# Six tiles of an input projection computed as fp32 products inside the stage that follows it

## The reference, cut to what matters

```python
def mixer(x, w_in, ...):               # names shortened
    parts = split(x @ w_in)            # 3360 columns: see below
    # a: spatial gating of two 256-wide parts       -> 256 columns
    # b: gated delta rule, 8 heads of 64, chunked   -> 512 columns
    # c: gated linear attention, 4 heads, chunked   -> 256 columns
    return concat([a, b, c]) @ w_out

def gated_deltanet(qkv, z, beta_logit, decay_logit, conv_w, a_log, dt_bias, norm_g):
    qkv = silu(causal_short_conv(qkv, conv_w))
    ...
    o = gated_delta_rule(q, k, v, log_g, beta)      # (I + L)^-1 per chunk, then a scan over chunks
    o = rms_norm_2(o, norm_g) * silu(z)             # z: 512 columns of x @ w_in
    return o
# the linear attention ends likewise: rms_norm_2(o, gla_norm_g) * silu(r), r: 256 columns of x @ w_in
```

## Time and profile before

| | |
|---|---|
| median of 3 runs | 3900.46 us (3897.31 to 3901.8) |
| the profiled execution | 3902.79 us |
| its span from first to last instruction | 3901.0 us |
| PE busy | 3753.3 us, 96% |
| DVE busy | 2088.4 us, 54% |
| ACT busy | 1354.9 us, 35% |
| granted PE clock, mean | 0.967 |
| DMA | 333.38 MB, mean 85 GB/s |

### The profile page before, as it was taken

One profiled execution on the slowest core, in us unless ns is written; L12 is line 12 of the kernel. 1 busy time (PEld: TensorE's weight loads), 2 busy tenths in 40 slices (PEclk: granted clock), 3 DMA queues, 4 the chain that ended last, 5 costly groups with the idle time before them and its releaser, 6 DMA issues.

```text
span 3901.0 us, 45251 instructions
## 1 busy us (share of the span) xinstructions
PE 3753.3 (96%) x18816; PEld 3126.8 (80%) x18816; DVE 2088.4 (54%) x3698; ACT 1354.9 (35%) x2084; POOL 86.1 (2%) x164
## 2 busy tenths in 40 slices
PE   8997999999999999999999979999999999799998
PEld 5985669999987778888887867888788878687886
...
PEclk9998999999999999999999968999999999789999
...
GB/s 220 151 57 1 22 22 133 125 127 127 106 70 33 38 88 96 97 111 97 97 97 86 85 20 44 92 97 97 86 97 97 97 87 86 29 39 87 97 98 81
DMA packets 92887, 333.38 MB, mean 85 GB/s; under 512 B 11364, under 2 KB 11532, under 8 KB 92428
## 3 DMA queue, kind: packets, MB, share of 16 engines
...
...
## 4 chain that ended last, share of the span: by engine, by line
PE 91%; DVE 5%; ACT 2%; issue 1%; DMA 0%; ACTq 0%; DVEq 0%; SPq 0%
PE PS L537 75%; PE PS L1093 2%; PE PS L539 2%; PE PS L1111 1%; PE PS L1639 1%; PE PS L1451 1%; PE PS L1078 1%; PE PS L994 1%; PE PS L1079 0%; PE PS L1081 0%; DVE H_r L719 0%; DVE XH L891 0%; PE PS L2339 0%; PE PS L2566 0%; PE PS L1422 0%
## 5 line engine op out<-in xcount | busy, mean ns | idle before, releaser
L537 PE MATMUL PS<-arena_r,ring_hi 128*128 128x512 f32 (+1 forms) x6124 | 2062.9, 376 | 22.5 <-DVE H_r L719 19.9
L537 PE MATMUL PS<-arena_r,ring_r 128*128 128x512 f32 (+1 forms) x4652 | 1740.2, 374 | 0.0
L537 PEld LDWEIGHTS PS<-arena_r,ring_hi 128*128 128x128 f32 x6124 | 1144.8, 188 | 203.2 <-issue 27.5
L537 PE MATMUL PS<-H_r,ring_hi 128*128 128x512 f32 (+1 forms) x3180 | 1190.1, 374 | 0.0
L537 PEld LDWEIGHTS PS<-arena_r,ring_r 128*128 128x128 f32 x4652 | 874.7, 188 | 129.1
L383 DVE TENSOR_TENSOR ring_r<-ring,ring_hi 128x1024 fp32r<-128x1024 f32 x514 | 627.1, 1222 | 655.1 <-ACT ring_hi L374 654.6
L374 ACT ACTIVATE ring_hi<-ring 128x1024 fp32r<-128x1024 f32 x514 | 541.4, 1055 | 876.9 <-DMA ring<-weights_dram 869.1
L537 PEld LDWEIGHTS PS<-H_r,ring_hi 128*128 128x128 f32 x3180 | 599.2, 188 | 92.8 <-issue 2.6
L1808 ACT ACTIVATE arena<-PS 128x512 f32<-128x512 f32 x88 | 52.6, 598 | 522.0 <-PE PS L537 522.0
L1257 DVE SCALAR_TENSOR_TENSOR XH<-PS,mods,XH 128x256 f32<-128x256 f32 (+1 forms) x168 | 79.4, 517 | 234.3 <-PE PS L537 219.8
L345 DVE CAST arena_r<-arena 128x512 fp32r<-128x512 f32 (+1 forms) x184 | 74.2, 403 | 196.6 <-ACT arena L1304 193.5
...
## 6 DMA issues: line engine op xcount, KB each, us to landing
...
```

What stands on the lines that cost most here:

```text
L537: ins = pe.matmul(PS[:, o.bank, 0:hi - lo], w[:, 0, :], x, **flags)
```

## The change

The six gate tiles leave `in_plan`, which now has 20 tiles; their weights stand in the stream behind it, ahead of the output projection's. They are never split: PE multiplies the raw fp32 slab with the raw fp32 input `X`, 48 products of 128x128 by 128x512 in each layer (`woven_pe`), in groups of 1 to 7 put between the steps of `form_pe`, `units_pe` and `solve_pe`. ACT copies each finished tile out of PSUM in six places (`woven_act`), and applies Silu in place during the scan (`woven_silu_act`), which needs one table load to Silu and one back. The bank numbers of several steps change so that banks 4, 6 and 7 are free for the new tiles, and some of these steps get a wait for a reader of their new bank. ACT and DVE no longer split the six slabs, and the first slabs of the output projection are split later: two high parts in `units_act`, one at the end of `solve_act`, two low parts at the start of `rec_dve`. The jobs beside the tiles of `in_plan` move to lower numbers. The same bytes are loaded.

```diff
 MIX_ORDER = [0, 1, 6, 7, 2, 3, 4, 5]
+WOVEN_COLS = [(2048, 2560), (3088, 3344)]
+WOVEN_BANKS = (4, 4, 6, 7, 6, 7)
+N_WOVEN = len(WOVEN_BANKS)
...
-                s += ftiles(w, (1408, 1536)) + ftiles(w, (512, 1024)) + ftiles(w, (1536, 2560)) + ftiles(w, (2576, 2832))
-                s += ftiles(w, (3088, 3344)) + ftiles(w, (0, 512)) + ttiles(w, (2832, 3088))
+                s += ftiles(w, (1408, 1536)) + ftiles(w, (512, 1024)) + ftiles(w, (1536, 2048)) + ftiles(w, (2576, 2832))
+                s += ftiles(w, (0, 512)) + ttiles(w, (2832, 3088))
+                for cols in WOVEN_COLS:
+                    s += ftiles(w, cols)
...
+WOVEN_SLABS = {i // SLAB for i, (w, k, c, n) in enumerate(stream()) if w in ("in0", "in1") and any(a <= c < b for a, b in WOVEN_COLS)}
+SPLIT_SLABS = [n for n in range(RAW_SLABS, N_SLABS) if n not in WOVEN_SLABS]
+SPLIT_NUMBER = {n: i + 1 for i, n in enumerate(SPLIT_SLABS)}
...
+        def next_split(n):
+
+            n += 1
+            while n in WOVEN_SLABS:
+                n += 1
+            return n
...
-                Splits.high += 1
+                Splits.high = next_split(n)
...
-            t += [ftile(x_x, LAT, "act", func_act(to_lat(zp[:, m, :]), ACT.Silu)) for m in range(4)]
             t += [ftile(x_x, LAT, "dve", copy_dve(to_lat(d))) for d in (qg, kg)]
-            t += [ftile(x_x, LAT, "act", func_act(to_lat(rg[:, m, :]), ACT.Silu)) for m in range(2)]
             t += [ftile(x_x, LAT, "act", func_act(to_lat(d), ACT.Gelu_apprx_tanh)) for d in (up_[:, 0, :], up_[:, 1, :], vp_[:, 0, :], vp_[:, 1, :])]
             t.append(ttile(x_x, range(NCT, NT), 2, "act", copy_act(lambda lo, hi: vg[:, lo // P - NCT, :])))
             banks.first = 0
+            assert Planned.at // SLAB in WOVEN_SLABS
+            Planned.at += SLAB * N_WOVEN
...
-            t[15]["beside_pe"] = lambda pe: turn_rows_pe(pe, l)
-            t[16]["beside_act"] = lambda act: (turned_rows_act(act), high_rows_act(act))
-            t[17]["beside_pe"] = lambda pe: turn_keys_pe(pe, l)
-            t[18]["beside_dve"] = lambda dve: (key_rows_dve(dve, l), low_rows_dve(dve))
-            t[20]["beside_pe"] = lambda pe: turn_values_pe(pe, l)
-            t[21]["beside_dve"] = value_rows_dve
+            t[14]["beside_pe"] = lambda pe: turn_rows_pe(pe, l)
+            t[15]["beside_act"] = lambda act: (turned_rows_act(act), high_rows_act(act))
+            t[15]["beside_pe"] = lambda pe: turn_keys_pe(pe, l)
+            t[16]["beside_dve"] = lambda dve: (key_rows_dve(dve, l), low_rows_dve(dve))
+            t[17]["beside_pe"] = lambda pe: turn_values_pe(pe, l)
+            t[18]["beside_dve"] = value_rows_dve
             return together(t, 4)
...
+        wv_ready, wv_out = signal("woven_tile_ready"), signal("woven_tile_out")
+        woven_dst = [zp[:, m, :] for m in range(4)] + [rg[:, m, :] for m in range(2)]
+
+        class Woven:
+
+            products = tiles = 0
+
+        def woven_pe(pe, n):
+
+            for _ in range(n):
+                tile, k = divmod(Woven.products, KD)
+                j = tile % N_WOVEN
+                w, last_of_slab = raw_tiles(pe, 1)
+                if k == 0 and WOVEN_BANKS[j] in WOVEN_BANKS[0:j]:
+                    before = max(i for i in range(j) if WOVEN_BANKS[i] == WOVEN_BANKS[j])
+                    pe.wait_ge(wv_out.sem, 2 * (tile - j) + before + 1)
+                ins = pe.matmul(PS[:, WOVEN_BANKS[j], :], w[:, 0, :], X[:, k, CTX:TOK], start=(k == 0), stop=(k == KD - 1))
+                if last_of_slab:
+                    ins.then_inc(wv_ready.sem, 1)
+                    Weights.used.append((wv_ready, tile + 1))
+                Woven.products += 1
+
+        def woven_copied_pe(pe, l, j):
+
+            pe.wait_ge(wv_out.sem, 2 * N_WOVEN * l + j)
+
+        def woven_act(act):
+
+            j = Woven.tiles % N_WOVEN
+            act.wait_ge(wv_ready.sem, Woven.tiles + 1)
+            nc.scalar.activation(woven_dst[j], PS[:, WOVEN_BANKS[j], :], ACT.Copy).then_inc(wv_out.sem, 1)
+            Woven.tiles += 1
+
+        def woven_silu_act(act, l, m):
+
+            if m == 0:
+                act.wait_ge(wv_out.sem, 2 * N_WOVEN * l + N_WOVEN)
+            nc.scalar.activation(woven_dst[m], woven_dst[m], ACT.Silu).then_inc(wv_out.sem, 1)
...
-        OUT_BANKS = (6, 0, 7, 1)
+        OUT_BANKS = (4, 0, 5, 1)
 
         def update_of(c):
 
-            return PS[:, 6 - 4 * (c % 2), 64 * (c // 2):64 * (c // 2) + 64]
+            return PS[:, 4 - 2 * (c % 2), 64 * (c // 2):64 * (c // 2) + 64]
 
...
             ins.then_inc(sg_z.sem, 1)
+            woven_pe(pe, 5)
             pe.wait_ge(sg_sq.sem, sg_sq.next("pe"))
...
             ins.then_inc(sg_t.sem, 1)
+            woven_pe(pe, 7)
             pe.wait_ge(sg_v.sem, sg_v.next("pe"))
...
             ins.then_inc(ga_kt.sem, 1)
+            woven_pe(pe, 1)
+            woven_copied_pe(pe, l, 2)
             pe.wait_ge(sg_tc.sem, sg_tc.next("pe"))
             pe.wait_ge(ga_ktc.sem, ga_ktc.next("pe"))
...
             ins.then_inc(sg_z.sem, 1)
+            woven_pe(pe, 2)
             pe.wait_ge(ga_state.sem, ga_state.next("pe"))
...
                 ins.then_inc(ga_s.sem, 1)
+            woven_pe(pe, 4)
             pe.wait_ge(ga_pt.sem, ga_pt.next("pe", 4))
...
             ins.then_inc(ga_o.sem, 1)
+            woven_pe(pe, 4)
...
         def units_act(act, l):
 
+            woven_act(act)
             act.wait_ge(sg_mean.sem, sg_mean.next("act"))
...
             nc.scalar.activation(kdt, PS[:, 5, :].rearrange("p (a b) -> p a b", a=4), ACT.Copy).then_inc(ga_ktc.sem, 1)
+            woven_act(act)
+            woven_act(act)
+            high_up_to(act, Splits.high + 1)
+            high_up_to(act, Splits.high + 1)
             act.wait_ge(ga_o.sem, ga_o.next("act"))
...
             def beta(p):
-                if p >= 2:
-                    pe.wait_ge(so_kb.sem, so_kb.at("pe", p - 2))
-                spread(pe, PS[:, 4 * (p % 2), :], "selp", P * p, mean_r).then_inc(so_beta.sem, 1)
+                spread(pe, PS[:, 0, :], "selp", P * p, mean_r).then_inc(so_beta.sem, 1)
...
             decays(0)
+            woven_pe(pe, 2)
             for p in range(4):
+                pe.wait_ge(so_kb.sem, so_kb.at("pe", p))
                 if p < 3:
                     beta(p + 1)
-                pe.wait_ge(so_kb.sem, so_kb.at("pe", p))
                 if p >= 1:
...
                 products(p, 3, qkv).then_inc(so_kq.sem, 1)
+                woven_pe(pe, 5 if p == 3 else 3)
...
-        EXP_BANKS = (2, 3, 6, 7)
+        EXP_BANKS = (2, 3, 2, 3)
         EXP_SPREADS = ((0, 1), (), (2,), (3,))
...
                 ins.then_inc(so_y.sem, 1)
+            woven_pe(pe, 1)
             pe.wait_ge(so_T.sem, so_T.next("pe"))
             for g in range(2):
...
                 ins.then_inc(so_z.sem, 1)
+                woven_pe(pe, 2)
                 for p in EXP_SPREADS[r]:
+                    if p == 1:
+                        pe.wait_ge(so_offv.sem, so_offv.at("pe", 1))
+                    if p >= 2:
+                        pe.wait_ge(re_qd.sem, re_qd.at("pe", p - 2))
                     spread(pe, PS[:, EXP_BANKS[p], :], "selp", P * p, exp_r, 64).then_inc(re_eg.sem, 1)
                 if r >= 1:
                     corner(r - 1)
...
                     nc.scalar.activation(pt_of(h).all, pt_of(h).all, ACT.Exp).then_inc(so_exp.sem, 1)
+                if p == 2:
+                    woven_act(act)
                 if p >= 2:
                     compact(act, p - 2)
...
+            woven_act(act)
             for r in range(4):
...
             so_top.advance("act", 4)
+            woven_act(act)
+            high_up_to(act, Splits.high + 1)
...
+                if n == 0:
+                    woven_copied_pe(pe, l, N_WOVEN)
...
                     nc.scalar.activation(uu[:, 256 * g:256 * g + 256], PS[:, 2 * g, 256:512], ACT.Copy).then_inc(re_u.sem, 1)
+                for m in range(2 * n, min(2 * n + 2, N_WOVEN)):
+                    woven_silu_act(act, l, m)
+                if n == 2:
+                    roots_table()
 
...
+            for _ in range(2):
+                split_up_to(dve, Splits.at + 1)
             dve.wait_ge(re_gtx.sem, re_gtx.next("dve"))
...
             (lo, hi), = LAT
+            dve.wait_ge(wv_out.sem, 2 * N_WOVEN * (l + 1))
             for k in MIX_ORDER[2:4]:
```

28 lines of the change are left out of this document (13 added, 15 removed).

## The result

| | before | changed |
|---|---|---|
| median (4 runs each, same chip) | 3900.16 us (3897.31 to 3901.8) | 3840.93 us (3838.91 to 3843.37) |
| the profiled execution / its span | 3902.79 / 3901.0 us | 3840.34 / 3838.6 us |
| granted PE clock, mean | 0.967 | 0.985 |

The ratio is 0.9848, with a 95% interval of 0.9836 to 0.986: 59.2 us faster. The forecast was 70.6 us faster, 3830, with 3808 to 3864 as its range. The projection gave what was forecast and the clock came up in most of the stage; one stretch in one layer cost more than the missing 11 us, and smaller gains elsewhere made up for a part of it.

What follows compares the result with a forecast made beforehand. PE was taken as the bound, busy 96% of the span, except where it waits. Projection -32.7 and stage -2.6 us a layer, doubled, gave -70.6: 3830 us from the median of 3900.46, range 3808 to 3864.

Steps and rivals of the forecast that it cites:

- the case that I held for likeliest: Whole kernel: the summed forecast, 3830 us by the median, own range 3822 to 3840; chance 0.50.
- the PE-bound one: Rival: PE bounds the stage between the projections, clock half in part; 3854 us, range 3842 to 3890; chance 0.18.
- a stage longer than 128 us: Sign of being wrong: the stage between input and output projections, expected at 118 to 124 us in each layer.
- the clock of the 32x32 part and the scan's first chunk: Signs expected in the profile: clock 0.50 in the 32x32 part, the scan's first chunk as short as its second.
- Projection, -65.3: Input projection: 144 fewer products a layer save 32.7 us each, 65.3 in both; 0 to 3 us of waits a layer.
- the rival that had the side work collide: Input projection: ACT's and DVE's jobs collide in six tiles fewer, costing 3 to 8 us a layer; 3842 us; chance 0.07.
- Price of a product, 0.887: Each woven raw fp32 product costs 0.887 us, bounds 0.887 and 1.89; 48 cost 42.6 us a layer at full clock.
- Form and units, -0.6: Form -0.3 us a layer (bounds -3 and +3), units and inverse -0.3 (bounds -1.5 and +1.5), DVE the bound.
- 32x32, +0.5: Solve's 32x32 steps: a woven product between them costs +0.5 us a layer, bounds -1.5 and +1.
- 64x64, +2: Solve's 64x64 part, PE-bound: eight woven products, first one or two steps at half clock; +2 us a layer, bounds -1 and +7.
- Scan, -4.5: Scan's first 9.94 us shrink at full clock by 4.5 us a layer, bounds 0 and -5; work put in there hidden.
- full clock all through: Rival: clock stays full through the whole stage, -7.3 us a layer there; 3820 us, range 3812 to 3824; chance 0.20.

Runs made afterwards that it cites:

- the gap alone: Changed kernel with two of the four woven products at the units' end moved behind the 32x32 products; 3846.93 us, ratio 0.9863 to the kernel before.
- one of eight: Changed kernel with seven of the eight products of each gate tile left out; 3839.51 us, ratio 0.9853 to the kernel before.
- the gap empty: Changed kernel with no woven products in the 64x64 part or behind the 32x32 products, and 12 at the units' end; 3845.82 us, ratio 0.9858.
- all moves: Changed kernel, six tiles: products moved from form's end behind the barrier, others into waits behind 32x32, in 64x64 and at the scan's start; 3826.07 us, ratio 0.9816.
- five tiles: As all moves, but five tiles woven, the sixth back in the projection, and only two products at the units' end; 3841.02 us, ratio 0.9841.

## Why the prediction was right, and where it was off

The total is in the range, but near the line between two cases: 3840.93 is just above the 3822 to 3840 of the case that I held for likeliest and just below the 3842 of the PE-bound one. By a sign that I had set myself, a stage longer than 128 us, I was wrong in layer 0, which took 133.6; the clock of the 32x32 part and the scan's first chunk did not come as listed either. That the total is no farther off is in part luck: form, units and the 32x32 part (5.3 us) and the stretch that no term covers (3.9 us) took back half of the 18.2 us that layer 0's 64x64 part and the two scans cost beyond the forecast.

**Projection, -65.3: right** (-65.2). The stretch is 109.3 us for 142, PE busy in 109.08 of it: no wait shows at tile 14, and the rival that had the side work collide is dead.

**Price of a product, 0.887: right.** At the units' end the group of two in the kernel with the gap alone, and the group of four in the changed kernel:

```profile
2287.98 1.98 PE L2134 MATMUL PS<-XH,ring 128*128 128x512 f32 x4
```

```profile
2283.93 3.70 PE L2134 MATMUL PS<-XH,ring 128*128 128x512 f32 x8
```

That is 0.86 us for each further product, and 0.26 for a group's tail; five products, 4.56 us above, agree. The other bound, 1.89 at half clock, was paid in layer 0's 64x64 part, two products in 3.78 us:

```profile
2296.53 3.78 PE L2134 MATMUL PS<-XH,ring 128*128 128x512 f32 x4
```

Over all 96 products the mean is 98.5 / 96 = 1.03 us.

**Form and units, -0.6: right in sum** (-1.6 and -1.1), with the clock at 1.00 in form and 0.96 to 1.00 in the units. The bound in form is another than I wrote: PE, busy 25.88 of 26.49 us, and not DVE. I had the barrier's delay, and took it for covered.

**32x32, +0.5: wrong sign** (-1.7, -1.1). I had expected half clock because only one product stands near. The clock came in at 1.00 and held: what counted was the four products at the units' end, which leave 0.66 us of PE's wait ahead of the first 32x32 product; the kernels with two there had 2.35 us of wait and lost the clock.

**64x64, +2, bounds -1 and +7: this is the term that failed** in layer 0, with +13.7; layer 1's +1.1 was within. I had read the danger right (a first step or two at half clock) and sized it wrong: I took the woven products for what brings a fallen clock back within a step or two. Two products in each cycle did not do so for 27 us here, and did within 5 us in the kernel with the gap alone; why is open.

**Scan, -4.5: mis-sized,** -1.3 in both layers. The clock falls once more behind the wait ahead of the scan, and two thirds of that stretch still run at 1.2 GHz (6.8 of 10.1 us, mean 0.66). With a product in each of the two waits it takes 7.8 us at full clock, one product included, so the 4.5 was the right size for a stretch that the change did not put in order. What I put in there (two low parts, Silu and its tables) was hidden: the rest of the scan has 19.8 us in both kernels.

The sum's error, 8.1 us in the profiled executions, is +11.7 for 64x64 in layer 0 and -0.9 in layer 1, +6.5 for the two scans, -5.3 for form, units and the 32x32 part of both layers, and -3.9 for the stretch that both kernels share. Of the rivals, "full clock all through" was right in layer 1 up to the scan; "PE-bound, half clock in part" describes layer 0.

The Trainium skill (TensorE: Matmul & The Clock Gate, Part 1) has the clock follow how busy PE has been. The falls right behind a wait are in its sense. Three readings here are not: layer 1 of the changed kernel kept its clock behind waits of the same sum, the clock fell once with PE 100% busy, and layer 0's 64x64 part was busy 29.60 of 30.47 us at a mean of 0.55. Where they differ, the measurement decides.

**Shown and open.** Shown by single changes: woven products hold up the clock (one of eight), and taking two of them from the units' end or from behind the 32x32 products brings it down in both layers (the gap alone, the gap empty). With all these places filled, one profiled execution had its whole stage at 1.00 (all moves). Argued, not shown: that it is PE's wait that brings the clock down. Each edit that opened a wait did so by taking 128x512 products out of it, so the rival that it is their thinning that counts is not told apart; the same holds for the wait ahead of the scan. The fall under a fully busy PE needed no wait. No run put such products into the waits of the kernel before and left the projection alone, which would price the clock by itself. Open: why layer 1 of the changed kernel came through about the same wait as layer 0, why the clock fell under a fully busy PE in one profile, why the same pairs had it back after 5 us in one kernel and 27 in another, and why executions of one kernel differ by 13.6 and 18.6 us (all moves, six and five tiles) when the whole stage depends on it.
